# Recurrent chunk products of an RWKV scan on one core: neighbouring 64x64 matmuls in all four quarters of the array in turn

## The reference

```python
def rwkv_scan(state0, terms, reverse, with_output):
    def step(S, inp):
        w_t, k_t, v_t, a_t, b_t = inp[-5:]
        sa = jnp.einsum('bhvk,bhk->bhv', S, a_t)
        S = S * w_t[:, :, None, :] + sa[..., None] * b_t[:, :, None, :] + v_t[..., None] * k_t[:, :, None, :]
        y_t = jnp.einsum('bhvk,bhk->bhv', S, inp[0]) if with_output else None
        return S, y_t
    S, ys = lax.scan(step, state0, xs, reverse=reverse)
```

## Time and profile before

| | us |
|---|---|
| median of 3 executions | 2997.34 (2997.01 to 3000.13) |
| the profiled execution, its own time | 2998.88 |
| the span in its profile | 2997.1 |
| first layer's chunks, first score to last state product | 622.5 to 838 |
| second layer's chunks | 1377 to 1582 |

### The profile page before, as it was taken

How to read it: one execution, slowest core, us unless ns; L and a number is a source line. 1 busy time by engine, 2 the same in 40 slices (tenths; PEclk the granted TensorE clock), 3 DMA queues, 4 the chain that set the end, 5 groups by cost and what they waited for, 6 DMA issues and landing times. The chain is left out here.

```text
span 2997.1 us, 47694 instructions
## 1 busy us (share of the span) xinstructions
PE 2592.3 (86%) x19606; PEld 1990.4 (66%) x19606; DVE 1407.2 (47%) x2317; ACT 936.9 (31%) x1510; POOL 206.8 (7%) x347
## 2 busy tenths in 40 slices
PE   5899998868868899895987799889999897899997
PEld 1277667658846666665885566558878565588885
DVE  1145551356663555336665666453332464533323
ACT  0233442211123344321112555442222345422221
POOL 0000000055200000005520000000000000000000
PEclk9989999789979899877998999899999998999998
DMA  8431111100001211110001212113333221133332
GB/s 323 118 72 50 29 36 49 32 2 3 3 15 43 68 46 36 50 46 2 3 3 43 77 57 63 43 56 98 98 90 96 85 67 57 57 97 98 96 91 72
DMA packets 300767, 185.10 MB, mean 62 GB/s; under 512 B 5650, under 2 KB 284708, under 8 KB 300460
## 3 DMA queue, kind: packets, MB, share of 16 engines
q1 hardware_dynamic: 293580, 166.79, 18.6%
q0 software_dynamic: 1808, 5.26, 1.1%
q10 hardware_dynamic: 5200, 10.49, 1.0%
HBM read 177.79 MB, written 4.71 MB: 61 GB/s over the span
## 5 line engine op out<-in xcount | busy, mean ns | idle before, releaser
L243 DVE TENSOR_TENSOR wlo<-wraw,whi 128x1024 fp32r<-128x1024 f32 (+1 forms) x276 | 333.5, 1208 | 598.6 <-ACT whi L236 597.6
L280 PE MATMUL PW<-hhi,whi 128*128 128x512 f32 (+1 forms) x1184 | 448.5, 379 | 65.3 <-DVE hlo L761 39.2
L281 PE MATMUL PW<-hhi,wlo 128*128 128x512 f32 (+1 forms) x1184 | 445.3, 376 | 0.0
L282 PE MATMUL PW<-hlo,whi 128*128 128x512 f32 (+1 forms) x1184 | 444.4, 375 | 0.0
L236 ACT ACTIVATE whi<-wraw 128x1024 fp32r<-128x1024 f32 (+1 forms) x276 | 288.3, 1045 | 313.7 <-PE PW L282 289.7
L280 PEld LDWEIGHTS PW<-hhi,whi 128*128 128x128 f32 x1184 | 225.9, 191 | 115.9 <-issue 49.7
L335 PE MATMUL PW<-hhi,whi 128*128 128x512 f32 (+1 forms) x640 | 242.8, 379 | 23.4 <-DVE hlo L734 18.8
L282 PEld LDWEIGHTS PW<-hlo,whi 128*128 128x128 f32 x1184 | 225.9, 191 | 40.3
L281 PEld LDWEIGHTS PW<-hhi,wlo 128*128 128x128 f32 x1184 | 226.3, 191 | 38.5
L337 PE MATMUL PW<-hlo,whi 128*128 128x512 f32 (+1 forms) x640 | 226.9, 355 | 0.0
L336 PE MATMUL PW<-hhi,wlo 128*128 128x512 f32 (+1 forms) x640 | 226.9, 355 | 0.0
(11 more groups left out here) (376 smaller groups left out, 4583.9 us busy)
## 6 DMA issues: line engine op xcount, KB each, us to landing
wraw<-in_w_in SPq DMA_DIRECT2D x68, 512.0 KB, 3.9
wraw<-in_ffn_w_gate SPq DMA_DIRECT2D x44, 512.0 KB, 3.8
wraw<-in_ffn_w_up SPq DMA_DIRECT2D x44, 512.0 KB, 3.8
wraw<-in_ffn_w_down SPq DMA_DIRECT2D x32, 512.0 KB, 3.7
mod_w<-in_mod_w SPq DMA_DIRECT2D x7, 2048.0 KB, 8.1
wraw<-in_attn_w_in SPq DMA_DIRECT2D x24, 512.0 KB, 3.7
mod_w<-in_mod_w ACTq DMA_DIRECT2D x5, 2048.0 KB, 19.8
wraw<-in_w_out SPq DMA_DIRECT2D x16, 512.0 KB, 3.7
```

Of the source, the lines that this page charges most:

```text
L243: dve.tensor_tensor(wlo[:, slot, 0:kb, :], wraw[:, slot, 0:kb, :], whi[:, slot, 0:kb, :].bitcast(F32), ALU.subtract).then_inc(S("w_split"), 1)
L280: pe.matmul(acc, whi[:, u % 2, k, :], rhi[:, k0 + k, s0:s1], start=a, stop=False)
L281: pe.matmul(acc, wlo[:, u % 2, k, :], rhi[:, k0 + k, s0:s1], start=False, stop=False)
L282: last_mm = pe.matmul(acc, whi[:, u % 2, k, :], rlo[:, k0 + k, s0:s1], start=False, stop=b)
```

## The change

In four places the order of the matmuls changes. A new generator `quarters()` gives the 16 units so that four neighbours lie in the four quarters of the array: (0,0), (1,1), (0,1), (1,0) as (`e_`, `pi`). The two scores and the carried-state products run over it once, and where the half-wise loops gave one semaphore increment for each half, there is now one for all 16. The own terms run over groups of four units: first the four first products, then the four accumulating ones, then, with an output, the same for the other two. The DVE therefore waits for all 16 products where it waited for one half and then for the other. The number of matmuls, their shapes and operands, the banks they write and all work of the other engines stay.

```diff
-            per = dict(exps=2, AR=2, BK=2, Lb=2, Lk=2, ..., gq=2, gqe=1, hy=2, chS=2, che=2)
+            per = dict(exps=2, AR=2, BK=2, Lb=1, Lk=1, ..., gq=1, gqe=1, hy=1, chS=2, che=2)
...
-                        v.wait_ge(sem[made], value(made, j, e_ + 1))
+                        v.wait_ge(sem[made], value(made, j, 1))
...
-                    v.wait_ge(sem["gq"], value("gq", j, pi + 1))
+                    v.wait_ge(sem["gq"], value("gq", j, 1))
...
+            def quarters():
+                for d in range(2):
+                    for hp in range(2):
+                        for e_, pi in ((0, 0), (1, 1), (0, 1), (1, 0)):
+                            yield d, hp, e_, pi, 4 * d + 2 * hp + e_, slice(64 * e_, 64 * e_ + 64), slice(64 * pi, 64 * pi + 64)
...
-                for half in range(2):
-                    for d in range(2):
-                        for hp, e_, pi, dh, re, rp in units(d):
-                            if e_ == half:
-                                a = (2 * d + hp) * 2 * CH
-                                ins = e.matmul(bank(bk + e_)[rp, a:a + 2 * CH], BK[re, d, hp, i, rp],
-                                               AR[re, d, hp, 0:Rk + 1:Rk, rp], start=True, stop=True)
-                    ins.then_inc(sem[made], 1)
+                for d, hp, e_, pi, dh, re, rp in quarters():
+                    a = (2 * d + hp) * 2 * CH
+                    ins = e.matmul(bank(bk + e_)[rp, a:a + 2 * CH], BK[re, d, hp, i, rp],
+                                   AR[re, d, hp, 0:Rk + 1:Rk, rp], start=True, stop=True)
+                ins.then_inc(sem[made], 1)
...
+                for d, hp, e_, pi, dh, re, rp in quarters():
+                    a = (2 * d + hp) * 2 * CH
+                    ins = e.matmul(bank(pi)[re, a:a + 2 * CH], AW[rp, dh, 1, :], MB[rp, dh, 2:0:-1, :],
+                                   start=True, stop=True)
+                ins.then_inc(sem["gq"], 1)
...
+                for group4 in itertools.batched(quarters(), 4):
+                    for d, hp, e_, pi, dh, re, rp in group4:
+                        e.matmul(own(d, hp, pi, re, 0), MB[rp, dh, 2, :], AW[rp, dh, 0, :], start=True, stop=False)
+                    for d, hp, e_, pi, dh, re, rp in group4:
+                        ins = e.matmul(own(d, hp, pi, re, 0), MK[rp, dh, 0, :], vv(d, hp, e_, rp), start=False, stop=True)
+                    if has_y(j):
+                        for d, hp, e_, pi, dh, re, rp in group4:
+                            e.matmul(own(d, hp, pi, re, 1), AW[rp, dh, 0, :], MB[rp, dh, 1, :], start=True, stop=False)
+                        for d, hp, e_, pi, dh, re, rp in group4:
+                            ins = e.matmul(own(d, hp, pi, re, 1), vv(d, hp, e_, rp), MK[rp, dh, 1, :], start=False, stop=True)
+                ins.then_inc(sem["hy"], 1)
```

More of the change, by code:

```diff
@@ L1 @@
+import itertools
 import math
@@ L1299, in has_y @@
                 return full or j >= 2
-            per = dict(exps=2, AR=2, BK=2, Lb=2, Lk=2, tA=1, tB=1, tK=1, mb=2, mk=2, aw=1, bh=1, kh=1, w1=1, w1e=1,
-                       T=12, Te=12, X=8, Xe=10, XT=10, XTe=12, xa=2, xae=2, gq=2, gqe=1,
-                       hy=2, chS=2, che=2)
+            per = dict(exps=2, AR=2, BK=2, Lb=1, Lk=1, tA=1, tB=1, tK=1, mb=2, mk=2, aw=1, bh=1, kh=1, w1=1, w1e=1,
+                       T=12, Te=12, X=8, Xe=10, XT=10, XTe=12, xa=2, xae=2, gq=1, gqe=1,
+                       hy=1, chS=2, che=2)
             sem = {nm: S(f"rw_{nm}") for nm in per}
@@ L1473, in dve_batch @@
                     if step == 0:
-                        v.wait_ge(sem["hy"], value("hy", j, 2))
+                        v.wait_ge(sem["hy"], value("hy", j, 1))
                     add_own(step)
@@ new lines, in pe_batch, with vv, own @@
+                ins.then_inc(sem["gq"], 1)
+                def vv(d, hp, e_, rp):
+                    return vtok[rp, T[d], (2 * hp + e_) * CH:(2 * hp + e_ + 1) * CH]
+                def own(d, hp, pi, re, what):
+                    a = 4 * CH * what + (2 * d + hp) * CH
+                    return bank(2 + pi)[re, a:a + CH]
+                for group4 in itertools.batched(quarters(), 4):
[8 more added lines that the diff above has]
+                            ins = e.matmul(own(d, hp, pi, re, 1), vv(d, hp, e_, rp), MK[rp, dh, 1, :], start=False, stop=True)
```

## The result

The changed kernel takes 2955.14 us (median of 4 runs, 2953.95 to 2958.56) against 2997.69 (2997.01 to 3000.13): ratio 0.9858, 95% interval 0.9841 to 0.9876, that is 42.5 us less. The profiled execution took 2955.72 us in its own time, with a span of 2953.9.

The account below looks back on a forecast made before the run. In the chunks PE's order of work was taken to bound the time, through DVE's 28.5 us of own-term waits. Terms 23.4 + 3.1 + 4.0 + 1.4 + 0.6 = 32.5 us gave about 2965, range 2949 to 2982.

Parts of the forecast that it names:

- likeliest case: Whole kernel: the forecast of about 2965 us, with its own range from 2957 to 2972; chance 0.51.
- it all comes out: Rival: quarters alone limit and the shorter batch falls out of step with low-clock stretches; 46 us, 2951; chance 0.12.
- own terms: Ten output batches: rotating 128 records at 18 ns each starts DVE's add 2.34 us earlier; 23.4 us, bounds 8.0 and 27.2.
- the clock: Five batches' scores at half clock after `rw_y_added`: shorter scores save 0.8 us each; 4.0 us, from 0 to 14.
- the cap: Own terms: DVE's add cannot start before its decay ends, no earlier than 687.01, so at most 2.78 us a batch.
- Carried-state products at nothing: Chunk batches: all 16 products ready after the same 1.14 us as the first half before, so no gain or cost.
- Step two: Scores between the two state steps, eight batches: 0.45 us shorter, of which 0.39 can be won; 3.1 us, lower bound 0.
- the clock takes it back: Rival, chunks: PE idles for a larger share, bringing more low-clock stretches; 2984, or 2976 in half the batches; chance 0.12.
- First batches and batches without output: Each layer's first-batch scores at half clock, 0.7 us each, 1.4 us; two batches without output, DVE's L1594 waits, 0.6 us.
- Feeding: Rival, own terms: PE's instruction issue limits records to 30 ns (2980) or 25 ns (2974); chance 0.17.
- Slower: Rival: two quarters work at a time and each quarter change shows its weight load; 15 us more, 3012; chance 0.04.
- no difference: Rival: order does not matter, the array overlaps no more than before; within 0.2%, 2991 to 3003; chance 0.04.

Follow-up runs that it names:

- run by unit: Against the changed kernel, each unit's four own-term products stay in a row and only whole units go round the quarters; 2976.44 us, ratio 0.9941.
- Half by half: Against the changed kernel, only the carried-state products' order and their signal go back to half-wise; 2962.4 us, ratio 0.9885.
- filled pair: Kernel before and changed kernel, each with three unread constant products in PE's idle time before eight batches' scores; 2979.88 and 2951.56 us.
- the rest alone: Against the kernel before, only the scores and carried-state products rotate, own terms keep the old order; 2978.23 us, ratio 0.9943.
- the own terms alone: Against the kernel before, only the own terms rotate over the quarters, scores and carried-state products stay half-wise; 2972.19 us, ratio 0.992.
- the filled kernel after: Changed kernel plus three unread constant products in PE's idle time ahead of eight batches' scores; 2951.56 us, ratio 0.985.

## Why the prediction was right, point by point

**The result** of 2955.1 lies in the range of 2949 to 2982 and 10 us under the forecast of 2965; it is 2 us below the likeliest case's own range (2957 to 2972), on the side of "it all comes out" (2951). Against a sum of 32.5 us the spans differ by 43.2. That the result is no further off is in part luck: four terms were too small by 14.6 us together (own terms 4.4, step one 2.4, the clock 6.5, the first batches 1.3), and the gaps, which the sum did not have, took 5.0 of that back.

**Own terms: the mechanism was right, the size too small.** Forecast 23.4 us with 18 ns a record, measured 14.4 ns and 27.8 us, the cap (the bound of 27.2 left out the last 0.06 of it). Only the quarters limit; the eleven records of the earlier trace rows in which I read 20 ns hold a start with two quarters and made the estimate too slow. The prediction named two reasons why four quarters never work at once: the four products of a unit in one quarter, and neighbours that share a row half. The run by unit (4.72 us) shows that the first alone does it.

**Carried-state products at nothing: wrong.** The step "a first half after 1.14 us, the same as all of it" held for DVE's copy (1.17 measured), but the step overlooked what starts behind them. Half by half, they cost 4.5 us in ten batches: the own terms' end and the first state step both come later. These 4.5 us are no further term; they stand inside the 27.8 and the 2.4.

**State steps.** Step two gave 2.6 us where 3.1 was forecast; the wait did not vanish but stands at 0.21. Step one was forecast at nothing and gave 2.4. Its wait was also one for products that queue behind the own terms, and PE now reaches them (684.80) before DVE's add (685.29); that was to be seen.

**The clock: right in kind, too small.** Forecast 4.0 of at most 14, measured 10.5 from the sum and 10.7 from the filled pair. The prediction took the shorter scores inside each low stretch; in fact the stretches themselves became fewer and shorter. The rival "the clock takes it back" went the other way.

**First batches and batches without output.** 2.7 instead of 1.4, and 0.9 instead of 0.6. In the first layer the full clock came back 3.0 us after the first score instead of 6.6, which was no part of the forecast.

**Feeding.** The rival had a form that did not come: no rate of 25 or 30 ns shows in any record. What came are stops of 0.4 to 1.2 us at the border of some packets, 5.0 us in all, a term that the sum lacked. "Slower" and "no difference" are refuted by the records.

**Sum.** 27.8 + 2.4 + 2.6 + 0.9 + 2.7 - 0.4 + 10.5 - 5.0 = 41.5, and 1.7 outside the chunks. Settled are the own terms, the order, the clock as a whole and where the gaps stand. Open is which part of the change took away which low stretch: with the rest alone they vanish in the first layer and with the own terms alone many stay, but their places hang on where PE's pauses fall, and no run separates that; nor does one show why a gap lasts 1.2 to 1.6 us beyond the landing of its packet.

## What to carry to other kernels

Many small products on parts of the array should change the part with each product, not with each group: a run of eight records in one quarter gives away most of what the other three could do (37 ns a record, against 14.4 in turn and 55 to 58 for one quarter by itself). Then ask what stands directly behind such a run, since its tail and all that queues behind it move too. And when PE becomes this dense, look at its idle times "issue" and at the instruction packets, before more work is put into making it denser.

## What the runs showed of the hardware that was not expected

- 128 records of 64x64 over four quarters start 14.4 ns apart (1.83 us), over two quarters 27.7 (3.52 us); one quarter takes 55 to 58 ns a record. Two column halves of the same row half work beside one another at the full rate of each.
- Records do not start in the order of the program across quarters (an own term starts at 684.77 with six of the 32 carried-state records before it still to start), but a run of eight for one quarter holds up the others, and one of four hardly does (4.72 us for 128 records against 1.04 for 64; in turn 1.83 and 0.89). PE seems to look ahead by a few records only; how many, no run measured.
- PE can run out of instructions: four to ten gaps of 0.3 to 1.4 us for a kernel, 3.0 to 8.2 us, at 7.2 to 8.8 ns an instruction, each ending 1.2 to 1.6 us after a 16 KB packet landed. All 52 stand at one place of a block of 256 instructions in each layer. A shift by 128 instructions moves them, one by 256 leaves them before the same records.
- Half a clock after short idles cost this kernel 15.8 us. A filler of 2.4 us (its length in the filled kernel after) ahead of eight batches' scores took the low stretches out of the chunks up to their last 3 us, though it adds work to PE.
